# Layer 0 of a two-layer hybrid decoder: all gate units in three float32r passes, and what is moved around them

## The reference

```python
z = x @ w_in[i]                                   # 1024 x 3328
q, k, v, u, g_attn, g_ssm = jnp.split(z, splits, axis=-1)
a_out = sliding_window_attention(q, k, v, attn_sinks[i], rel_bias)
s_out = s5_mixer(u, ...)                          # complex-diagonal scan, GELU, GLU
merged = (sigmoid(g_attn) * (a_out @ w_branch_attn[i])
          + sigmoid(g_ssm) * (s_out @ w_branch_ssm[i]))
x = layer_norm(DEEPNORM_ALPHA * x + merged @ w_out[i], ...)
```

## Time and profile before

| | us |
|---|---|
| median of 3 runs | 1609.08 (1606.87 to 1609.2) |
| the profiled execution | 1609.16 |
| its span, first to last instruction | 1607.3 |
| TensorE busy | 1570.6 (98%) |
| VectorE busy | 1354.6 (84%) |
| ScalarE busy | 999.9 (62%) |
| GpSimd busy | 149.8 (9%) |

### The profile page before, as it was taken

How to read it: one execution, slowest core, us unless ns; L and a number is a source line. 1 busy time by engine, 2 the same in 40 slices (tenths; PEclk the granted TensorE clock), 3 DMA queues, 4 the chain that set the end, 5 groups by cost and what they waited for, 6 DMA issues and landing times.

```text
span 1607.3 us, 24068 instructions
## 1 busy us (share of the span) xinstructions
PE 1570.6 (98%) x9028; PEld 1332.7 (83%) x9028; DVE 1354.6 (84%) x1300; ACT 999.9 (62%) x913; POOL 149.8 (9%) x157
## 2 busy tenths in 40 slices
PE   8999999999999999999999999999999999999996
PEld 6889799999899978888888888888888888888884
DVE  8797856655687788999998999998999998999998
ACT  7345444334546437776777777777677677767763
POOL 2000139940300000000000000000000000000000
PEclk9999999999999999999999999999999999999998
DMA  7535855554444568999999999999999999999993
GB/s 225 162 107 183 301 180 192 185 183 132 130 132 148 200 230 297 360 372 359 361 369 334 351 369 370 352 366 334 351 371 360 354 377 332 345 377 364 360 361 124
DMA packets 169448, 456.55 MB, mean 284 GB/s; under 512 B 7638, under 2 KB 60919, under 8 KB 168872
## 3 DMA queue, kind: packets, MB, share of 16 engines
q1 hardware_dynamic: 168472, 450.87, 78.1%
q0 software_dynamic: 768, 4.75, 0.8%
q10 hardware_dynamic: 144, 0.05, 0.0%
HBM read 453.02 MB, written 2.62 MB: 283 GB/s over the span
## 4 chain that ended last, share of the span: by engine, by line
PE 86%; DVE 8%; issue 3%; DMA 1%; ACT 1%; SPq 0%; DVEq 0%; ACTq 0%
PE psum L735 20%; PE psum L737 20%; PE psum L736 20%; PE psum L742 6%; PE psum L744 6%; PE psum L743 6%; PE psum L845 4%; DVE wl L466 2%; PE psum L1199 1%; PE psum L871 1%; ACT wh L460 1%; PE psum L802 1%; DMA ring<-in_w_pg 1%; DVE hid L2190 1%; DMA ring<-in_w_in 1%
## 5 line engine op out<-in xcount | busy, mean ns | idle before, releaser
L466 DVE TENSOR_TENSOR wl<-ring,wh 128x2048 fp32r<-128x2048 f32 x269 | 609.3, 2287 | 67.0 <-ACT wh L460 63.2
L460 ACT ACTIVATE wh<-ring 128x2048 fp32r<-128x2048 f32 x307 | 581.7, 1920 | 126.3 <-PE psum L737 78.4
L736 PE MATMUL psum<-wl,xgh 128*128 128x512 f32 x896 | 349.2, 390 | 0.0
L735 PE MATMUL psum<-wh,xgh 128*128 128x512 f32 x704 | 282.0, 401 | 1.0 <-DVE xgl L2174 0.5
L737 PE MATMUL psum<-wh,xgl 128*128 128x512 f32 x704 | 274.9, 390 | 0.0
L736 PEld LDWEIGHTS psum<-wl,xgh 128*128 128x128 f32 x896 | 168.5, 188 | 32.4
L735 PE MATMUL psum<-wh,hidh 128*128 128x512 f32 x440 | 172.7, 393 | 3.7 <-DVE wl L466 2.8
L736 PE MATMUL psum<-wl,hidh 128*128 128x512 f32 x448 | 174.4, 389 | 0.0
L737 PE MATMUL psum<-wh,hidl 128*128 128x512 f32 x440 | 171.4, 390 | 0.0
L466 DVE TENSOR_TENSOR wl<-ring,wh_spare 128x2048 fp32r<-128x2048 f32 x72 | 164.5, 2284 | 3.0 <-ACT wh_spare L460 3.0
L735 PEld LDWEIGHTS psum<-wh,xgh 128*128 128x128 f32 x704 | 132.2, 188 | 33.6 <-DVE wl L466 5.5
(11 more groups left out here) (435 smaller groups left out, 2769.5 us busy)
## 6 DMA issues: line engine op xcount, KB each, us to landing
ring<-in_moe_gu SPq DMA_DIRECT2D x224, 1024.0 KB, 7.2
ring<-in_moe_dn SPq DMA_DIRECT2D x112, 1024.0 KB, 7.3
ring<-in_w_in SPq DMA_DIRECT2D x25, 1024.0 KB, 5.4
ring<-in_w_gu SPq DMA_DIRECT2D x22, 1024.0 KB, 5.1
ring<-in_w_dn SPq DMA_DIRECT2D x11, 1024.0 KB, 4.9
ring<-in_w_out SPq DMA_DIRECT2D x8, 1024.0 KB, 6.2
ring<-in_w_pg SPq DMA_DIRECT2D x8, 1024.0 KB, 5.2
ring<-in_w_ba SPq DMA_DIRECT2D x4, 1024.0 KB, 5.1
```

Of the source, the lines that this page charges most:

```text
L460: eng.activation(parts(u)[0], ring[:, ring_slot(u), :], ACT.Copy).then_inc(hi_ready, 1)
L466: eng.tensor_tensor(lo, ring[:, ring_slot(u), :], hi.bitcast(F32), ALU.subtract).then_inc(lo_ready, 1)
L735: pe.matmul(dst, ah, bh, start=first, stop=False, skip_group_check=True)
L736: pe.matmul(dst, ah, bl, start=False, stop=False, skip_group_check=True)
```

## The change

1. `FIRST_SPLIT` goes from 9 to 5: gate units 5 to 8 of layer 0 are split too. The places of the high parts in layer 0 are a table of their own, `GATE_HI`.
2. `make_turns` for layer 0 goes from VectorE to GpSimd, with `turns_ready`; its scratch is slot 5 of the ring, so ScalarE waits for it before it puts unit 6's high part there.
3. SP issues unit 1 ahead of the state maps and the two bias tables.
4. The bias products go from units 1 and 2 to units 2 and 3; `copy_rows` follows the copies of q.
5. x0h is copied after the first shift; the values are copied before the keys; TensorE does `local_products` before `turn_values`.
6. On VectorE both halves of `output_powers` come before xIl, and the new subtractions are set between the scans; later in the mixer layer 0 takes the order of layer 1 for units 14 and 15.

```diff
-FIRST_SPLIT = 9
+FIRST_SPLIT = 5
...
-HI_PLACE = ({i: p for i, p in (EARLY_HI | LATE_HI).items() if i >= FIRST_SPLIT}, EARLY_HI | LATE_HI)
+GATE_HI = {5: "ring4", 6: "ring5", 7: "early", 8: "ring4", 9: "ring5", 10: "ring4", 11: "turns"}
+HI_PLACE = (GATE_HI | LATE_HI, EARLY_HI | LATE_HI)
...
                     u += 1
-                    if u == 1:
+                    if u == 2:
                         sp.dma_start(raw.rearrange("p a b c -> p (a b c)"), bc_in[0]).then_inc(raw_dma, 16)
                         sp.dma_start(relb_sb[0:BUCKETS + 1], relb).then_inc(table_dma, 16)
                         sp.dma_start(hot_sb[0:BUCKETS + 1], hot_in).then_inc(table_dma, 16)
-                    if u == 2:
                         small_loads()
                     if u == RING:
                         skew_bias()
...
-                            if u in (1, 2) and k % 4 == 2:
-                                bias_row_of(4 * (u - 1) + 2 * t + k // 4)
+                            if u in (2, 3) and k % 4 == 2:
+                                bias_row_of(4 * (u - 2) + 2 * t + k // 4)
...
-                    turn_values(), local_products(0), input_states(0), scores(0)
+                    local_products(0), turn_values(), input_states(0), scores(0)
...
                     shift_inputs(lambda d, s: act.activation(d, s, ACT.Copy), g, (0, 1) if l else range(4), shifted_ready[0])
-                    if l == 0:
-                        copy_rows(g)
+                    if l == 0 and g == 0:
+                        act.wait_ge(xT_dma, 16)
+                        act.wait_ge(xT_rest, 16)
+                        act.activation(x0h[:], xT[:], ACT.Copy).then_inc(x0_hi, 1)
                 for g in (2, 3):
                     src = group(g)
                     act.activation(qT[:, 2 * (g - 2):2 * (g - 1), :], src, ACT.Copy, scale=HD ** -0.5).then_inc(qk_ready, 1)
                     act.wait_ge(qk_ready, 4 * l + g - 1)
                     act.nop().then_inc(g_free[g % 2], 1)
+                    if l == 0:
+                        copy_rows(g - 2)
+                        if g == 3:
+                            act.wait_ge(turns_ready, 1)
                     early_hi(3 + g)
                 if l == 0:
                     copy_maps(0)
-                    act.activation(x0h[:], xT[:], ACT.Copy).then_inc(x0_hi, 1)
+                act.activation(vt.rearrange("p a b -> p (a b)"), group(4)[:, 1, :], ACT.Copy).then_inc(v_ready, 1)
                 for kv in range(2):
...
             pool.wait_ge(decay_ready, 1)
+            pool.wait_ge(powers_ready, 1)
+            make_turns(pool, c.link, (ring[:, 5, 0:256], ring[:, 5, 256:512]), 0)
+            pool.nop().then_inc(turns_ready, 1)
...
                     output_maps(dve, link, 0, [v[:, n:n + 256] for v in (scratch_a, scratch_b) for n in (0, 256)])
-                    make_turns(dve, link, (scratch_a[:, 0:256], scratch_b[:, 0:256]), 0)
...
-                        if l:
-                            dve.wait_ge(turns_ready, l)
+                        dve.wait_ge(turns_ready, l + 1)
...
-                    output_powers(dve, link, 0, (scratch_a[:, 0:512], scratch_b[:, 0:512]), 8, (0,))
+                    output_powers(dve, link, 0, (scratch_a[:, 0:512], scratch_b[:, 0:512]), 8, (0, 8))
                     dve.wait_ge(x0_hi, 1)
                     dve.tensor_tensor(xIl[:], xT[:], x0h[:].bitcast(F32), ALU.subtract).then_inc(x0_lo, 1)
-                    scan_states(0), logits(0)
-                    normalise(0), scan_states(1)
-                    output_powers(dve, link, 0, temps, 8, (8,))
+                    early_lo(5), early_lo(6)
+                    scan_states(0), logits(0), early_lo(7)
+                    normalise(0), scan_states(1, 8)
...
-                if l == 1:
-                    early_lo(14), gated(0), gated(1), early_lo(15)
-                else:
-                    gated(0), gated(1), early_lo(14)
+                early_lo(14), gated(0), gated(1), early_lo(15)
                 dve.wait_ge(s_ready, 2 * (l + 1))
                 gated_lo(0), gated_lo(1)
-                if l == 0:
-                    early_lo(15)
```

More of the change, by code:

```diff
@@ L1399, in _ @@
                 ins.then_inc(qk_ready, 1)
-                act.activation(vt.rearrange("p a b -> p (a b)"), group(4)[:, 1, :], ACT.Copy).then_inc(v_ready, 1)
                 act.wait_ge(qk_ready, 4 * l + 3)
```

## The result

The changed kernel takes 1631.72 us (median of 4, 1630.74 to 1632.05); the kernel before, beside it, 1608.38 us. The ratio is 1.0145 (95% interval 1.0128 to 1.0163). The forecast was 1630.8 within 1622 to 1637. The profiled execution has a span of 1629.9 us, 22.6 more than before.

A forecast was written before the change was run, and what follows sets the result against it. The prediction took TensorE, 86% of the chain, as the bound. From 1609.2 us it added 17.8 up to unit 5 (18.2 + 1.7 - 2.1) and 3.8 at the mixer's end: 1630.8, range 1622 to 1637.

The forecast's parts named there:

- Unit 1: Start of layer 0's mixer: loading it earlier gains 1.9 us, lost again as TensorE waits for ScalarE from 33.5 to 35.4.
- Bias rows: Before turn_maps: the last four rows are copied after unit 3, so TensorE waits 2.6 us.
- The copy of unit 6: In turn_maps: ScalarE's copy awaits a load landing at 62.75, ahead of the map copies; TensorE stands 15.2 us; turn_maps +18.2.
- Clock: After the long stall in turn_maps: TensorE runs slow for a while, +1.7 us, bounds 0 and twice that.
- Values: Before the values' turn: copying values first, with local_products between, removes the 2.13 us wait, -2.1 us.
- Units 5 to 8: Gate units in three passes: 5.4 us less TensorE work, all spent by the first softmax and unit 9, so +0.
- GLU: Late in the mixer: the GLU product's second half waits 2.5 us for a bank; +3.8 in all by the first branch product.
- Turn table on GpSimd: Before the scans: takes 11.1 us off VectorE, which idles there anyway, so buys nothing; table done at 48.8.

The follow-up runs named there:

- unit6_ahead: The changed kernel with the load of unit 6 issued ahead of the bias round trip instead of behind it; ratio to the kernel before 1.0037.
- copy6_behind: The changed kernel with ScalarE's copy of unit 6 behind the map copies, keys and values, and VectorE's subtraction of unit 6 inside the first scan; ratio 1.0068.
- hole_filled_34: The changed kernel with 34 blank float32 products, which nobody reads, in TensorE's queue at the place of the 13.5 us hole in turn_maps; ratio 1.0132.
- split_alone: The kernel before with only the first split unit at 5, the new table of places and VectorE's subtractions for units 5 to 8; ratio 1.0121.
- attended_first: The changed kernel with ScalarE copying the attended rows before unit 10's high part in layer 0, not after it; ratio 1.0095.
- mended_turns_on_vector: The changed kernel with its early and later waits in layer 0 taken away by reordering, and layer 0's turn table back on VectorE; ratio 0.9979.

## Why the prediction was right, step by step

- **Unit 1** no longer waits; its 32 products and unit 0's are one stretch. The gain was foretold to be lost behind ScalarE's shifts: wait 33.5 to 35.4, measured 2.28 us to 35.66.
- **Bias rows:** 2.6 foretold, 2.53 measured.
- **The copy of unit 6:** landing foretold at 62.75, copy begun 62.91; TensorE starts again at 65.36 (65.2). The length of the hole was 15.2 in the sum and is 13.49, because the clock was low already from 48 us on (0.68 and 0.50 in the slices from 48 to 52), so the four groups ahead of it took 3.4 us and not 1.9, and they began 0.4 us later than in the sum. That cost nothing, since they ran inside the wait. The experiments leave this step as the cause: undoing either half of it (unit6_ahead, copy6_behind) undoes the hole.
- **Clock:** 1.7 taken, 1.5 by hole_filled_34. Right in size, and by the path taken: the transposes behind the wait at 1.2 GHz (0.50), 3.67 us and not 2.12. That the same happens behind short waits was not in the sum.
- **Values:** the 2.13 us wait is gone; split_alone, which keeps the old order, still has it (2.14). Unit 5 started at 83.05, foretold 83.2.
- **Units 5 to 8:** the first softmax's turn was foretold, in the new clock, at 101.1 and came at 101.15; unit 9 at 121.4 and came at 121.72. The split's gain was spent as described, 2.2 us at the softmax and 2.8 at unit 9; attended_first gives the second back.
- **GLU:** 2.5 foretold, 2.44 measured. Missing from the sum was a slow clock behind this wait, 0.78, 0.50 and 0.87 in the slices from 150 to 156 us, a loss of (0.22 + 0.50 + 0.13) x 2 = 1.7 us. The first branch product starts at 162.77, not 161.6, 1.2 us late. Of these, 0.5 were there when the wait ended (150.49, foretold 150.0); the other 0.7 are what is left of the 1.7, since TensorE waited 1.03 us before that product where the sum had some 2. The prediction gives 143.8 for this product with no working of the last step, so part of how close it came is luck. This slow clock, at nothing in the sum, is the term that was mis-sized; I had put one only behind the long hole.
- **Turn table on GpSimd:** "buys nothing" holds for this kernel, where VectorE idles 15 us ahead of the first scan. The table ended at 44.7, not 48.8. What the step left out is that GpSimd slows VectorE down (below); where VectorE is the bound the move is worth 3.5 us and not 11.1.

Predicted were 21.6 us more; the span has 22.6 more and the medians 23.3. At the mark it is 23.2: the 21.6, the 1.2 above and 0.4 between the first branch product and the mark.

## What to carry to other kernels

A call that does nothing under one setting comes alive under another: before changing such a number, write down for each queue what then stands behind the new wait, and what the thing waited for is queued behind in turn (here a weight load behind a store that waits for the same engine). Work taken off the busiest engine is worth only what the second and third engine let through: of 5.4 us of TensorE time some 2 arrive even in the best order found. And price a new wait of some 2.5 us at its length plus up to 1.7, since a slow clock may follow it.

## What the runs showed of the hardware

**A wait of 2 to 3 us may lower TensorE's clock, and the place tells more than the length.** After the 2.53 us wait at 46 and the 2.44 us wait at 148 the granted clock fell to 0.50 in the changed kernel; after those of 2.28 us at 33, 2.19 at 99 and 2.76 at 119 it did not. Over all the kernels of this case that have such a wait it fell behind the one for the bias rows (2.5 us) in seven of seven, behind the one in the GLU product (2.4) in seven of eight, behind the one for the softmax (2.2) in three of six, behind the one before unit 9 (2.8) in two of six, and behind the one before the fifth bias product (1.6 to 2.3) in one of seven, where the wait was the shortest, 1.61 us (hole_filled_34). Each of these falls costs 1.6 to 1.7 us by its slices. The Trainium skill, page TensorE: Matmul & The Clock Gate, section Part 1: The HAM clock gate, says that an idle array falls to 1.2 GHz, and that one kernel may show a different number of slow products at its start from run to run. The rows agree with the first; for the second, the six executions of unit6_ahead differ in their mean clock, 0.988 to 0.994. No run here shows what decides it.

**GpSimd slows VectorE beside it.** The turn table on GpSimd takes 26.2 us, first and last instruction (timeline of GpSimd, after):

```profile
18.46 0.12 POOL L490 MEMSET arena<- 128x16 f32 x1
...
43.93 0.77 POOL L506 TENSOR_TENSOR arena<-arena,ring 128x256 f32<-128x256 f32 x1
```

Beside it VectorE's operations on 128 x 32 elements, with both inputs in SBUF, grew to as much as 0.65 us (timeline of VectorE, after), where each of the same series took 0.19 before (second fence):

```profile
35.94 0.65 DVE L1791 TENSOR_TENSOR small<-small 128x32 f32<-128x32 f32 x1
...
42.11 2.74 DVE L567 COPY arena<-arena 64x256 f32<-64x256 f32 x4
```

```profile
32.72 0.19 DVE L1783 TENSOR_TENSOR small<-small 128x32 f32<-128x32 f32 x1
...
35.61 1.25 DVE L566 COPY arena<-arena 64x256 f32<-64x256 f32 x4
```

The map copies at the end of output_maps end at 44.9 and not at 36.9: of the 11.1 us taken off VectorE 8.0 came back as slower work, 3.1 were left, which mended_turns_on_vector confirms with 3.5. In that kernel and in split_alone, with the table on VectorE, the same operations take 0.19 us again. GpSimd is held up as well: between 21.8 and 29.8 us its operations on 128 x 64 elements took 0.90 to 1.03 us beside VectorE's long ones, while the 128 x 128 ones right behind them took 0.40. The Trainium skill, page SBUF — State Buffer, section Who interferes with whom, has the two engines lock each other out over a shared pair of ports. The rows agree, and more strongly than I had drawn from the GpSimd side alone: the many short operations on VectorE grow most for their length, as if each waited for one of GpSimd's; that reading is argued, no run here separates it.
